# K pages transposed in 32x32 blocks on VectorE, four samples at a time, in a decoder-layer kernel on one core

## What is computed

```
def page_step(state, phys):            # one page of each of the 8 samples, newest first
    o_acc, carry = state
    kp = cache_k[phys]; vp = cache_v[phys]
    zp = sb_logits(q, kp, sb_bias)     # q.k * scale + bias
    o_p, carry = sb_block(zp, True, vp, carry)
    return (o_acc + o_p, carry), None
# sb_block: log_om = log_sigmoid(-z); suffix = reverse cumsum(log_om) - log_om + carry
#           a = exp(log_sigmoid(z) + suffix);  o = a @ v;  carry += sum(log_om)
```

## Time and profile before

| | |
|---|---|
| median of 3 runs | 1241.01 us (1239.83 to 1242.74) |
| the profiled execution, its time | 1240.57 us |
| its span in the profile | 1238.9 us |
| busy in the span: PE, DVE, POOL, ACT | 1129.2, 628.8, 408.1, 399.6 us |
| mean granted TensorE clock | 0.965 |

### The profile page before, as it was taken

One profiled execution on the slowest core, in us unless ns is written; L12 is line 12 of the kernel. 1 busy time (PEld: TensorE's weight loads), 2 busy tenths in 40 slices (PEclk: granted clock), 3 DMA queues, 4 the chain that ended last, 5 costly groups with the idle time before them and its releaser, 6 DMA issues.

```text
span 1238.9 us, 25950 instructions
## 1 busy us (share of the span) xinstructions
PE 1129.2 (91%) x9815; PEld 989.1 (80%) x9815; DVE 628.8 (51%) x853; ACT 399.6 (32%) x626; POOL 408.1 (33%) x341
## 2 busy tenths in 40 slices
PE   6679999989887899899979887899999999999997
PEld 2358879867656677667769866899999999999996
DVE  0463633555534776566469554854554002554543
ACT  2532332324434554554441344412121111211121
POOL 0133343424322253334433102333333333332330
PEclk9879999989978999999989999999999999999998
DMA  9526685855899699989853131332222222222222
GB/s 363 176 85 236 222 314 199 315 179 192 284 358 340 203 339 309 357 302 348 270 207 121 35 118 53 103 103 68 85 76 76 79 93 86 83 78 66 64 64 76
DMA packets 126409, 220.69 MB, mean 178 GB/s; under 512 B 9935, under 2 KB 68564, under 8 KB 126308
## 3 DMA queue, kind: packets, MB, share of 16 engines
q1 hardware_dynamic: 103010, 146.10, 34.4%
q0 software_dynamic: 20480, 67.13, 15.4%
q10 hardware_dynamic: 2818, 6.13, 1.4%
HBM read 213.52 MB, written 5.80 MB: 177 GB/s over the span
## 4 chain that ended last, share of the span: by engine, by line
PE 77%; DVE 10%; DMA 5%; ACT 3%; issue 2%; SPq 2%; ACTq 0%; POOLq 0%; POOL 0%; DVEq 0%
PE ps L512 36%; PE ps L1547 14%; PE ps L1628 8%; PE ps L573 4%; PE ps L1653 4%; DMA k_page<-in_cache_sb_k 3%; PE ps L1685 3%; PE ps L1503 2%; DVE h_lo L417 2%; DVE run L1328 1%; DVE aw L1334 1%; PE ps L356 1%; DMA v_late<-in_cache_sb_v 1%; PE ps L1664 1%; DVE r_sum L675 1%
## 5 line engine op out<-in xcount | busy, mean ns | idle before, releaser
L468 POOL TENSOR_TENSOR w_lo<-w_raw,w_hi 128x2048 fp32r<-128x2048 f32 (+3 forms) x49 | 192.5, 3930 | 397.6 <-ACT w_hi L445 358.5
L512 PE MATMUL ps<-h_hi,w_hi 128*128 128x288 f32 x832 | 179.7, 298 | 11.6 <-DVE h_lo L417 8.4
L512 PE MATMUL ps<-h_lo,w_hi 128*128 128x288 f32 x832 | 178.6, 297 | 0.0
L512 PE MATMUL ps<-h_hi,w_lo 128*128 128x288 f32 x832 | 178.5, 296 | 0.0
L1628 PE MATMUL ps<-cc,k_page 128*128 128x128 f32 x1024 | 145.1, 295 | 32.4 <-DVE kT L1301 12.9
L1628 PEld LDWEIGHTS ps<-cc,k_page 128*128 128x128 f32 x1024 | 121.1, 150 | 54.7 <-issue 37.9
L445 ACT ACTIVATE w_hi<-w_raw 128x2048 fp32r<-128x2048 f32 (+3 forms) x47 | 77.9, 1662 | 257.8 <-PE ps L512 227.2
L609 POOL DMA_DIRECT2D v_late<-in_cache_sb_v x168 | 90.3, 537 | 177.1 <-issue 109.2
L512 PEld LDWEIGHTS ps<-h_hi,w_hi 128*128 128x128 f32 x832 | 134.5, 189 | 12.8 <-issue 9.3
L1301 DVE COPY kT<-ps 128x512 f32<-128x512 f32 x128 | 87.8, 691 | 95.2 <-PE ps L1628 94.8
L512 PEld LDWEIGHTS ps<-h_lo,w_hi 128*128 128x128 f32 x832 | 134.5, 189 | 0.0
(11 more groups left out here) (253 smaller groups left out, 1853.5 us busy)
## 6 DMA issues: line engine op xcount, KB each, us to landing
k_page<-in_cache_sb_k SPq DMA_DIRECT2D x256, 256.0 KB, 5.2
v_late<-in_cache_sb_v POOLq DMA_DIRECT2D x168, 256.0 KB, 5.2
v_early<-in_cache_sb_v POOLq DMA_DIRECT2D x88, 256.0 KB, 4.9
mw_raw<-in_w_in SPq DMA_DIRECT2D x12, 1024.0 KB, 5.8
w_raw<-in_w_gate SPq DMA_DIRECT2D x11, 1024.0 KB, 5.3
w_raw<-in_w_up SPq DMA_DIRECT2D x11, 1024.0 KB, 5.3
w_s<-in_w_in SPq DMA_DIRECT2D x4, 1536.0 KB, 12.8
w_raw<-in_w_down SPq DMA_DIRECT2D x8, 768.0 KB, 4.4
```

The costliest lines, as they stand in the source:

```text
L468: return nc.gpsimd.tensor_tensor(w_lo[s][:, ks, :], w_raw[s][:, ks, :], w_hi[s][:, ks, :].bitcast(F32), ALU.subtract)
L512: op = nc.tensor.matmul(ps[:, 2 * t + hf, 0:b - a], weights[s][:, k, t * P:(t + 1) * P], x[:, k0 + k, a:b], start=begin and k == ks[0] and ...
```

## The change

Two groups of 16 chunks take the place of four of 8; a group serves four samples, and a chunk holds two pages of each. K is no longer transposed on PE. A page of K goes to one quadrant of 32 partitions (sample g to partitions 32g to 32g+31, four rows of 2 KB in each partition), so eight DMAs of 256 KB with 32 partitions on the SBUF side fill `k_page`, in two halves of four pages. DVE transposes blocks of 32x32 from `k_page` straight into `kT`, four instructions for a chunk, and the queries are laid out to fit (`q_bd` by quadrants, `q_new` for the new tokens). The copies of K on ACT and DVE are gone. Scores use 16 matmuls of 256 columns into two banks in place of 8 of 512 into one; sums use 16 of 256 columns in place of 32 of 128. Sigmoids are four of 256 columns, the scan two of 256, in place. Other banks are assigned to side work.

```diff
-        def k_pages(sp, C):
-            for q in range(8):
+        def k_pages(eng, C):
+            for p in range(2):
                 if C:
-                    sp.wait_ge(s_ktr, 8 * C + q - 7)
-                load_page(sp, C, q, ck, k_page[:, q:q + 1, :], s_kp[q // 2])
+                    eng.wait_ge(s_ktr, 4 * (C - 1) + 2 * p + 2)
+                for g in (0, 2, 1, 3):
+                    page = page_of(eng, C, 4 * p + g)
+                    eng.dma_start(k_page[32 * g:32 * g + 32, p, :, :],
+                                  ck[0, bass.ds(page, 1)].rearrange("o (a i) h d -> i (o a) (h d)", a=4))\
+                        .then_inc(s_kp[2 * p + g // 2], 16)
+        def v_step(n):
+            first, late = 8 * LAST, 8 * LAST + V2
+            return (n - V1) // 8 + 2 if n < first else LAST + 1 if n < late else (n - V2) // 8 + 2
@@ gpsimd
             for C in range(CHUNKS):
-                if 0 < C < CHUNKS - 1:
-                    v_pages(pool, C + 1, range(2) if C + 1 < LAST else range(4))
                 if 2 * C + 4 < TILES:
                     tile_lo(2 * C + 4)
...
-                if C < CHUNKS - 1:
-                    v_pages(pool, C + 1, range(2, 8) if C + 1 < LAST else range(4, 8))
+                v_pages(pool, C + 2)
                 if 2 * C + 5 < TILES:
                     tile_lo(2 * C + 5)
@@ scalar
-            def copy_k(C):
...
+                for hh in range(2):
+                    nc.scalar.activation(beta_s[:, hh, 0:w], ps[:, 2 + hh, 0:w], ACT.Sigmoid,
+                                         scale=SB_SCALE, bias=bias_s[:, hh:hh + 1])
@@ vector
-                    nc.vector.tensor_copy(kT[:, q // 4, :, (q % 4) * P:(q % 4 + 1) * P], tiled(ps[:, q % 3, :]))\
-                        .then_inc(m_["k_copied_d"], 1)
+            def transposes(C):
+                slots = kT[:, :, :].rearrange("p b (x i) -> p x b i", i=32)
+                for p in range(2):
+                    dve.wait_ge(s_kp[2 * p], 32 * (C + 1))
+                    dve.wait_ge(s_kp[2 * p + 1], 32 * (C + 1))
+                    if p == 0 and C:
+                        dve.wait_ge(m_["score"], (PER + 1) * ((C - 1) // PER) + (C - 1) % PER + 2)
+                    for a in (0, 2):
+                        nc.vector.transpose(slots[:, 4 * p + a:4 * p + a + 2, :, :],
+                                            k_page[:, p, a:a + 2, :].rearrange("p a (b j) -> p a b j", j=32))\
+                            .then_inc(s_ktr, 1)
@@ tensor
-            def k_transposes(C):
...
             def scores(C):
-                pe.wait_ge(m_["k_copied_a"], 4 * C + 4)
-                pe.wait_ge(m_["k_copied_d"], 4 * C + 4)
-                        op = nc.tensor.matmul(ps[32 * j:32 * j + 32, 3, :], q_bd[:, s, j, :], kT[:, s, j, :],
-                                              start=s == 0, stop=s == 1)
+                pe.wait_ge(s_ktr, 4 * C + 4)
+                for hh in range(2):
+                    for e in range(2):
+                        for k in range(4):
+                            block = 2 * (4 * hh + k) + e
+                            op = nc.tensor.matmul(ps[32 * k:32 * k + 32, 2 + hh, 0:2 * P],
+                                                  q_bd[:, block, :], kT[:, block, :],
+                                                  start=e == 0, stop=e == 1)
```

More of the change, by code:

```diff
@@ L618, in v_pages, with page_of @@
[L618 to L629, removed]
+        def page_of(eng, C, q):
+            n = 32 * (4 * (C // PER) + q % 4) + 30 - 2 * (C % PER) + q // 4
+            return eng.value_load(ptb[0:1, n:n + 1], min_val=0, max_val=N_POOL - 1)
@@ L1035, in copy_weights @@
+                for hh in range(2):
+                    nc.scalar.activation(beta_s[:, hh, 0:w], ps[:, 2 + hh, 0:w], ACT.Sigmoid,
+                                         scale=SB_SCALE, bias=bias_s[:, hh:hh + 1])
+                for hh in range(2):
+                    op = nc.scalar.activation(om_s[:, hh, 0:w], ps[:, 2 + hh, 0:w], ACT.Sigmoid,
+                                              scale=-SB_SCALE, bias=bias_s[:, 2 + hh:3 + hh])
+                op.then_inc(m_["om"], 1)
             def copy_weights(S, new):
@@ L1167, in _ @@
             copy_weights(0, True)
-            sample_sigmoids(1, SEQ)
+            sample_sigmoids(1, 2 * P)
             tile_hi(2)
-            for g in range(GROUPS):
-                group(g, g == GROUPS - 1)
-            act.wait_ge(m_["rows_copied"], GROUPS)
+            for g in range(SG):
+                group(g, g == SG - 1)
+            act.wait_ge(m_["rows_copied"], SG)
             hi_parts(act, "out", pT[:, T_A:T_A + KC, :], G_ATT, range(KC), KC)
@@ new lines, in weights @@
+            def weights(S, w):
+                G, k = divmod(S, PER + 1)
+                R = RUNS * G + (1 if k == 0 else 1 + 3 * k)
+                dve.wait_ge(m_["om"], S + 1)
+                if k == 0:
+                    nc.vector.memset(om_s[:, :, w:w + 1], 1.0).then_inc(m_["run"], 1)
+                    dve.wait_ge(m_["run"], R)
+                for hh in range(2):
+                    om_ = om_s[:, hh, 0:w][:, ::-1]
+                    nc.vector.tensor_tensor_scan(om_, om_, om_, om_s[:, hh, w:w + 1], ALU.mult, ALU.bypass)\
+                        .then_inc(m_["run"], 1)
+                dve.wait_ge(m_["run"], R + 2)
+                nc.vector.tensor_tensor(beta_s[:, :, 0:w], beta_s[:, :, 0:w], om_s[:, :, 1:w + 1], ALU.mult)\
@@ L1367, in group @@
             def group(g, last):
[L1368 to L1369 removed]
+                for c in range(PER):
+                    C, u = PER * g + c, PER * g + c - LAST
                     if 2 * C + 1 < TILES:
@@ L1372, in group @@
                     if C + 1 < CHUNKS:
-                        copy_k(C + 1)
-                    if c == 7 and not last:
+                        transposes(C + 1)
+                    if c == PER - 1 and not last:
                         queries(g + 1)
+                        new_queries(g + 1)
                     if 2 * C + 2 < TILES:
@@ L1434, in _ @@
             evac(0)
-            weights(1, 3, SEQ)
-            for g in range(GROUPS):
-                group(g, g == GROUPS - 1)
+            weights(1, 2 * P)
+            for g in range(SG):
+                group(g, g == SG - 1)
             grant(s_free["out"], 2)
```

342 lines of the change are left out of this document (165 added, 177 removed).

## The result

The changed kernel takes 1296.55 us in the median (1288.24 to 1300.14, 4 runs) beside 1241.88 us of the kernel before on the same chip. The ratio is 1.043 (95% interval 1.037 to 1.048). The prediction was 1252 us with a range up to 1286: the direction was right, the time lies outside the range.

The account below looks back on a forecast made before the run. PE was taken to bound the early chunks and, narrowly ahead of DMA, the late ones; after the change DMA would bound late. Early -16, late +30, start -2 made +12 on 1240.6 us: 1252 us, range 1192 to 1286.

Parts of the forecast that it names:

- The transposes on DVE: In the chunks, each DVE transpose of K was put at 1.23 us, from the copy's rate.
- The third rival: Late chunks: transposes take 2.56 us each, DVE is busy as long as DMA; about 1270 us, chance 5%.
- K on one half: K page loads to 32 partitions: 14.4 GB/s a busy engine instead of 23.1, so 0.43 us more a page.
- The 189 GB/s: Skill's rate for 32 partitions: a K page takes 1.39 us, the late stretch 40 us more, the sum 1292 us.
- The late DMA term: Late chunks: DMA busy 275 + 65 - 15 = 325 us, at share 0.96 makes 339 us, 30 us more.
- relief: Late chunks: slower K leaves less crowding of the DMA engines, which gives back 15 us of busy time.
- The first rival: K pages to different quadrants overlap, extra under 0.2 us a page: late stretch -23 us, 1200 us in all, chance 28%.
- The early chunks: Early stretch: second tiles 9 us, one step without it 3, group boundary 4; together 16 us less of 223.
- The 31 us: Early chunks: if POOL's queue holds nothing up, chunks come near 16.2 us instead of 19.4, worth 31 us.
- The start: Before the chunks: shorter query copies and earlier readiness of the new tokens' weights give back 2 us.
- The end: Group ends: a product and three sums replace a copy; fewer but longer boundaries were left at nothing.
- The second rival: Halves of `k_page` wait for each other, a turn of 18.9 us: 40 us on top, 1292 us, chance 14%.

Follow-up runs that it names:

- e7_stride4: `e2_tl_first` with each K page on every fourth partition instead of 32 neighbours, not the reference's layout: 1214.72 us, 0.976 of the kernel before.
- e6_64part: `e2_tl_first` with each K page on 64 neighbouring partitions of one half, two rows each, not the reference's layout: 1293.97 us, 1.034 of the kernel before.
- e5_no_alternate: `e2_tl_first` with K pages requested in sample order 0, 1, 2, 3, so two in a row reach the same half: 1300.10 us, 1.046 of the kernel before.
- e1_k128: The changed kernel with every K page landing on all 128 partitions, not the reference's layout: 1237.81 us, 0.996 of the kernel before.
- e12_k128_tl: The changed kernel with the edits of both `e1_k128` and `e2_tl_first`: 1203.49 us, 0.967 of the kernel before.
- e2_tl_first: The changed kernel with the load of the second tile's low part issued ahead of V requests on POOL: 1276.89 us, 1.029 of the kernel before.
- e4_interleave: `e2_tl_first` with each K page requested as two 128 KB pieces that go to the two halves in turn: 1277.38 us, 1.028 of the kernel before.

## Why the prediction was right in direction and wrong in size

**The transposes on DVE: right.** 1.23 us worked out, 1.218 measured, x128. The third rival (slow transposes) is out.

**K on one half: the mechanism right, its price alone nearly so.** 14.4 GB/s a busy engine came from a store; K alone gives 240 / (16 x 1.07) = 14.0. The prediction ascribed it to the number of partitions, and that is wrong: it is the half (`e7_stride4`, `e6_64part`). For this kernel both words gave the same number. The 189 GB/s that the prediction cites from the Trainium skill was too low for these requests, a row of 256 KB pages that take the halves in turn and run at 240. That the estimate made from it, 1292 us, lies 5 us from the measured time is luck.

**The late DMA term, "275 + 65 - 15 = 325, +30": the step that failed.** I priced K's own extra and let the rest get quicker, a "relief" of 15 us. The trace shows the opposite. Between the marks the busy time rose by 350 - 260 = 90 us. K packets of the late stretch went from 90.0 to 132.3 ns, which for its 20335 packets over 16 engines makes 20335 x 42.3 / 16 = 54 us. V packets, untouched, went from 187.9 to 229.4: 10377 x 41.5 / 16 = 27 us; packets of 1 KB give 3 more. So K's term was a little too large (65 for 54) and V's had the wrong sign (-15 for +27): 50 us were forecast where 84 to 90 came. My share of 0.96 for a full stretch was low (0.99), which hid some 10 us of it. The first rival, that pages overlap, had a grain of truth worth some 21 us (`e5_no_alternate`), not the 0.43 us a page that it needed. Its price was off as well: with K at its old speed it had 275 / 0.96 = 286 us, and `e1_k128` takes 296.6, with 271 us of DMA work but a share of only 0.91.

**The early chunks, "9 + 3 + 4 = 16": mis-sized, it measured 5.** The cause was named, V's requests ahead of the low part, but the working compared one chunk with the one before, as if the requests began when they did. They begin when V's sums free the places, and the sums stand behind the very tile that waits: a circle of 21.8 us, 6 of them at half clock. The 31 us named for a queue that holds nothing up came out to the microsecond, in part by luck, since neither level did (chunks of 20.7 and 17.6 us where 19.4 and 16.2 were named), and only with K on 128 partitions; with K on quadrants the engines, 0.92 busy as forecast, leave 8.

**The start: -2 forecast, -5 measured**; the 3 us between are not explained. **The end:** 3.5 us at the last chunks and 4.9 us in the stages without pages were forecast at nothing. The first stay with the change where no request is slow: from the scores of chunk 31 to the output projection `e12_k128_tl` takes 19.7 us, the changed kernel 19.3, the kernel before 15.8. The second go with the granted clock. From the output projection to the end, before and then after:

```profile
627.70:1238.90 611.20, 578.51 (x4342) 563.66 (x4340) 306.29 (x355) 143.58 (x182) 188.45 (x48) 0.99 0.26 85
678.80:1294.90 616.10, 583.13 (x4341) 567.90 (x4341) 307.05 (x359) 143.50 (x182) 187.78 (x47) 0.98 0.26 84
```

PE is busy for 4.6 us more with the same matmuls. The trace's clock records have 0.50 for 17 us of this stretch before and for 29 us after; in `e12_k128_tl` and `e2_tl_first` it is 18 us, and both take 611.7 us. Why the clock was low for longer in this execution is not shown.

**The sum.** Forecast -16 + 30 - 2 = +12; measured -5 + 61 - 5 + 5 = +56, where 61 is the late stretch with the end of the chunks. Of the 44 us between them the late stretch has 31, the early 11, start and end 2. The second rival gave nearly the measured time, 1292 us, for a reason that did not hold: the DMA engines were not waiting for turns, they were full. It became true only where the engines had been relieved (`e4_interleave`).

**What is shown and what is argued.** Shown: one edit of the destination takes 56.5 us out of the late stretch, and the same edit alone puts 68 us into the kernel before; POOL's order is worth 31 us with K on all partitions. Argued: that V is slower because its packets meet K's on the shared engines; it follows V's packet times, which move with K's destination in every run, but how the two meet is not visible. No kernel here beats the one before with the change's layout. The 1203 us of `e12_k128_tl` say what such a layout would be worth, if one can be found whose requests reach both halves and still leave each sample in its own quadrant. Transposing on DVE in the early chunks alone, and on PE in the late ones, was not tried.

## What to carry to other kernels

Before choosing a layout for a compute instruction, ask which partitions each single DMA request then reaches: neighbours in one half load at 240 GB/s, the same 32 partitions' worth spread over both halves at 367. Price such a slowdown for everything that shares the DMA engines, not for the slowed requests alone. And when a request queue and an engine wait for each other once a turn, add up the whole circle instead of comparing one start with its old start.

## What the runs showed of the hardware

- V's packets, on all 128 partitions and on another queue, slow down by 27% in the mean (184.4 to 234.8 ns) when K's go to one half at a time.
- PE's tile behind a wait of 3.67 us ran at a granted clock of 0.50 for some 6 us, and the scores behind a wait of 13.6 us, at 0.50 too, took 3.64 in place of 1.93 us: a wait can cost more than itself.
- DVE's scan of 256 columns lasts 0.73 us, but one that ran beside POOL's low parts (159.30 to 163.96 us) lasted 4.75. Of the 68 scans of this line, the 57 that met no low part took 0.75 us at most, and the eight that took over 2 us all met one:

```profile
159.77 4.75 DVE L1331 TENSOR_TENSOR_SCAN om_s<-om_s 128x256 f32<-128x256 f32 x1 [2.52 <-ACT om_s L1045]
```

The Trainium skill, page "SBUF — State Buffer", section "Who interferes with whom", says that a VectorE instruction with two inputs in SBUF contends with a GpSimd instruction that reads SBUF. The scan, both of whose inputs are `om_s`, agrees.
